# Starting the input projection in two halves of the channels, on six open sums

## The reference, cut to what matters

```python
mod = (jax.nn.silu(c) @ w_ada[l] + b_ada[l])[:, None, :]
sh_m, sc_m, g_m, sh_f, sc_f, g_f = jnp.split(mod, 6, axis=-1)
h = rmsnorm(x, norm_mix_w[l]) * (1.0 + sc_m) + sh_m
z, xbc, dt, q, k, v = jnp.split(h @ w_in, SPLITS, axis=-1)
```

## Time and profile before

| | us |
|---|---|
| median of three runs | 1695.97 |
| the profiled execution | 1696.15 |
| its span in the trace | 1694.4 |
| TensorE busy in the span | 1593.2 |
| the first matmul of the projection starts at | 62.93 |
| the first matmul of unit 2 starts at | 95.56 |

### The profile page before, as it was taken

One profiled execution on the slowest core, in us unless ns is written; L12 is line 12 of the kernel. 1 busy time (PEld: TensorE's weight loads), 2 busy tenths in 40 slices (PEclk: granted clock), 3 DMA queues, 4 the chain that ended last, 5 costly groups with the idle time before them and its releaser, 6 DMA issues.

```text
span 1694.4 us, 23175 instructions
## 1 busy us (share of the span) xinstructions
PE 1593.2 (94%) x9153; PEld 1412.9 (83%) x9153; DVE 994.3 (59%) x1603; ACT 651.8 (38%) x1143; POOL 453.6 (27%) x274
## 2 busy tenths in 40 slices
PE   4899998899998888789999999999999999999996
PEld 3689897689996666668899999999889989989875
DVE  3765416732115777654776666666466687667834
ACT  4531223321114666644332232224444454445532
POOL 0121124332201000365743333333621121112232
PEclk8899999899999999999999999999999999999998
DMA  9545110231214222327522222222364435544442
GB/s 326 198 163 199 38 28 1 57 89 38 67 53 155 101 101 77 124 87 205 203 68 67 66 62 63 63 78 73 99 188 124 133 103 167 160 135 122 149 164 70
DMA packets 163858, 189.09 MB, mean 112 GB/s; under 512 B 7851, under 2 KB 126868, under 8 KB 163731
## 3 DMA queue, kind: packets, MB, share of 16 engines
q1 hardware_dynamic: 148074, 148.89, 28.1%
q10 hardware_dynamic: 10300, 21.01, 4.1%
q0 software_dynamic: 5376, 17.71, 3.0%
HBM read 170.48 MB, written 17.11 MB: 111 GB/s over the span
## 4 chain that ended last, share of the span: by engine, by line
PE 81%; DVE 10%; ACT 3%; issue 3%; DMA 2%; POOL 1%; ACTq 0%; DVEq 0%; SPq 0%; POOLq 0%
PE PS L727 17%; PE PS L728 16%; PE PS L729 16%; PE PS L1188 4%; PE PS L1190 4%; PE PS L1189 4%; PE PS L650 4%; PE PS L1117 2%; PE PS L1118 2%; PE PS L1119 2%; PE PS L1046 2%; PE PS L985 2%; DVE y_new L1666 1%; PE PS L740 1%; DMA weights_raw<-in_w_up_dram 1%
## 5 line engine op out<-in xcount | busy, mean ns | idle before, releaser
L2347 POOL TENSOR_TENSOR weights_lo<-weights_raw,weights_hi 128x1024 fp32r<-128x1024 f32 x103 | 267.6, 2601 | 696.4 <-ACT weights_hi L1876 532.3
L727 PE MATMUL PS<-h_hi,weights_hi 128*128 128x384 f32 x1280 | 433.9, 339 | 3.3 <-DVE h_lo L1279 2.9
L728 PE MATMUL PS<-h_lo,weights_hi 128*128 128x384 f32 x1280 | 431.4, 337 | 0.0
L729 PE MATMUL PS<-h_hi,weights_lo 128*128 128x384 f32 x1280 | 431.3, 337 | 0.0
L1876 ACT ACTIVATE weights_hi<-weights_raw 128x1024 fp32r<-128x1024 f32 x202 | 213.2, 1058 | 159.1 <-PE PS L1190 97.5
L727 PEld LDWEIGHTS PS<-h_hi,weights_hi 128*128 128x128 f32 x1280 | 241.7, 189 | 11.9 <-issue 11.7
L728 PEld LDWEIGHTS PS<-h_lo,weights_hi 128*128 128x128 f32 x1280 | 241.7, 189 | 0.1
L729 PEld LDWEIGHTS PS<-h_hi,weights_lo 128*128 128x128 f32 x1280 | 241.6, 189 | 0.0
L1188 PE MATMUL PS<-weights_hi,g_hi 128*128 128x512 f32 x396 | 159.3, 402 | 8.9 <-POOL g_lo L2485 5.5
L1190 PE MATMUL PS<-weights_hi,g_lo 128*128 128x512 f32 x396 | 157.4, 397 | 0.0
L1189 PE MATMUL PS<-weights_lo,g_hi 128*128 128x512 f32 x396 | 156.6, 396 | 0.0
(11 more groups left out here) (389 smaller groups left out, 2465.3 us busy)
## 6 DMA issues: line engine op xcount, KB each, us to landing
weights_raw<-in_w_up_dram SPq DMA_DIRECT2D x88, 512.0 KB, 3.9
weights_raw<-in_w_down_dram SPq DMA_DIRECT2D x66, 512.0 KB, 4.4
w_ada_unit<-in_w_ada_dram SPq DMA_DIRECT2D x32, 512.0 KB, 5.4
weights_raw<-in_w_in_dram SPq DMA_DIRECT2D x24, 512.0 KB, 5.4
weights_raw<-in_w_out_dram SPq DMA_DIRECT2D x24, 512.0 KB, 4.0
w_ada<-in_w_ada_dram SPq DMA_DIRECT2D x4, 2048.0 KB, 16.7
k_cache<-in_cache_k_dram SPq DMA_DIRECT2D x8, 1024.0 KB, 7.7
v_cache<-in_cache_v_dram SPq DMA_DIRECT2D x8, 1024.0 KB, 5.5
```

The lines of the kernel that those rows point to most:

```text
L727: pe.matmul(out, wh, xh, start=(i == 0), stop=False)
L728: pe.matmul(out, wh, xl, start=False, stop=False)
L729: mm = pe.matmul(out, wl, xh, start=False, stop=(i == n - 1))
L2347: mark(gp.tensor_tensor(WL[n % 3][:, :], WR[:, n % 3, :], WH[n % 3][:, :].bitcast(F32), ALU.subtract), "w_lo")
```

## The change

- Units 0 and 1 are computed by a new `first_units(g, half)`: for each block k of half the channels the three matmuls of unit 0 and the three of unit 1, waiting for each h_lo block by its own count (`MOD_NO`). So six sums are open at once, in six banks (`FIRST_BANKS`), and are completed in a second pass over channels 512 to 1023.
- The products and sums of quarters 2 and 3 (`ada_products(2)`, `(3)`, `ada_sum(2)`, `(3)`) stand between the three groups of the first half and no longer before all of the projection. `late_pair(0)` to `(3)` stand in the second half.
- The products of quarters 0 and 1 stand among the last turns of x: after the seventh and after the ninth tile.
- VectorE copies the first tile out before it scales tiles 3 to 5, and three tiles (1 to 3), no longer two, before it scales the last three.
- Modulation goes half by half over all groups on both engines, the sample tile too in two halves of the channels. `w_hi(2)` stands between the halves.

```diff
+            for j in range(6):
+                x_turn(j)
+            pe.wait_ge(*once("cond_T"))
+            setup_turns()
+            x_turn(6)
             ada_products(0)
+            x_turn(7)
+            x_turn(8)
             ada_products(1)
-            pe.wait_ge(sem("xT_dve"), NT)
-            pe.wait_ge(sem("xT_act"), NT)
             ada_sum(0)
             ada_sum(1)
-            ada_products(2)
-            ada_products(3)
-            ada_sum(2)
-            ada_sum(3)
...
+            def first_units(g, half):
...
+                for k in HALVES[half]:
+                    if g < 2:
+                        pe.wait_ge(sem("mod_lo"), MOD_NO[g, k])
+                    elif k == 4 * half:
+                        pe.wait_ge(sem("mod_lo"), MOD_NO["sample", half])
+                    for n in range(2):
...
+                        pe.matmul(bank, WH[n][:, ws], HH[:, k, cols], start=(k == 0), stop=False)
+                        pe.matmul(bank, WH[n][:, ws], HL[:, k, cols], start=False, stop=False)
+                        mm = pe.matmul(bank, WL[n][:, ws], HH[:, k, cols], start=False, stop=(k == KT - 1))
...
+            first_units(0, 0)
+            ada_products(2)
+            first_units(1, 0)
+            ada_sum(2)
+            ada_products(3)
+            first_units(2, 0)
+            ada_sum(3)
+            first_units(0, 1)
             late_pair(0)
             late_pair(1)
-            for g in range(NG):
-                in_group(0, g)
-                in_group(1, g)
-                if g < 2:
-                    late_pair(2 + g)
+            first_units(1, 1)
+            late_pair(2)
+            first_units(2, 1)
+            late_pair(3)
...
             x_norm(0)
+            x_out(0)
             x_norm(1)
-            for j in range(3):
+            for j in range(1, 4):
                 x_out(j)
             x_norm(2)
...
-            x_turned_out(0)
+            for j in range(3):
+                x_turned_out(j)
             x_stats(2)
-            x_turned_out(1)
-            x_turned_out(2)
+            for j in range(3, 8):
+                x_turned_out(j)
             w_hi(0)
+            x_turned_out(8)
             w_hi(1)
```

More of the change, by code:

```diff
@@ L461, in build, with proj_bank @@
         HALVES = [range(4), range(4, KT)]
-        MOD_ACT = [[(g, k) for g in range(NG) for k in HALVES[0]],
-                   [(g, k) for g in range(2) for k in HALVES[1]], [(2, k) for k in HALVES[1]]]
-        MOD_DVE = [[(0, k) for k in HALVES[0]], [(1, k) for k in range(2)], [(0, k) for k in HALVES[1]],
-                   [(1, k) for k in range(2, KT)], [(2, k) for k in range(KT)]]
-        MOD_HI = {gk: i + 1 for i, gk in enumerate(sum(MOD_ACT, []))}
-        MOD_LO = [[i for i, (g, _) in enumerate(sum(MOD_DVE, [])) if g == group][-1] + 1 for group in range(NG)]
-        MOD_LO[2] += 1
+        MOD_BLOCKS = [(g, k) for half in range(2) for g in list(range(NG)) + ["sample"]
+                      for k in (HALVES[half] if g != "sample" else [half])]
+        MOD_NO = {gk: i + 1 for i, gk in enumerate(MOD_BLOCKS)}
+        FIRST_BANKS = [0, 1, 2, 7, 5, 6]
+        ADA_BANKS = [4, 5, 4, 3]
+        def proj_bank(q):
+            return FIRST_BANKS[q] if q < 6 else q % 3
         SUMMED = [MIXED.index(("d", 0, FT - 1)), MIXED.index(("d", 0, 2 * FT - 1))]
@@ L734, in late_pair @@
                 pe.wait_ge(sem(f"pair_in{i % 2}"), 32 * (i // 2 + 1))
-                if i % 4 == 0 and i:
-                    pe.wait_ge(sem("ada_row"), 4 + i // 4)
+                if i % 4 == 0:
+                    pe.wait_ge(*((sem("ada_row"), 4 + i // 4) if i else (sem("ada_sum_out"), 4)))
                 for t in range(2):
@@ L1265, in scale_cols, with modulate @@
                                             op0=ALU.add, op1=ALU.mult), name)
-            def modulate(blocks):
-                for g, k in blocks:
+            def modulate(g, ks):
+                for k in ks:
                     n = 3 if g < 2 else 2
@@ L1279, in modulate, with modulate_sample, sample_lo @@
                     mark(ve.tensor_scalar(lo, x, SCOL[:, 0, k, 0:1], None, ALU.add), "mod_lo")
+            def modulate_sample(half):
+                ks = slice(4 * half, 4 * half + 4)
+                x4 = XIN[:, NPT, ks, :].rearrange("p k (b t) -> p k b t", b=NB)
+                ch(ve.tensor_tensor(x4, x4, AM[:, ks, 1:NCOND].unsqueeze(3).to_broadcast([P, 4, NB, TS]), ALU.mult))
+                out(ve.tensor_tensor(x4, x4, SCOL[:, 0, ks, 1:NCOND].unsqueeze(3).to_broadcast([P, 4, NB, TS]), ALU.add),
+                    "mod_sample")
+            def sample_lo(half):
+                ks = slice(4 * half, 4 * half + 4)
+                ve.wait_ge(sem("mod_hi"), MOD_NO["sample", half])
+                mark(ve.tensor_tensor(HL[:, ks, SEQ:T], XIN[:, NPT, ks, :], HH[:, ks, SEQ:T].bitcast(F32), ALU.subtract),
+                     "mod_lo")
             x_norm(0)
+            x_out(0)
             x_norm(1)
-            for j in range(3):
+            for j in range(1, 4):
                 x_out(j)
             x_norm(2)
-            for j in range(3, 6):
-                x_out(j)
+            x_out(4)
+            x_out(5)
             setup_cols()
-            for j in range(6, NT):
-                x_out(j)
+            x_out(6)
             ada_row(0)
+            x_out(7)
+            x_out(8)
             ada_row(1)
@@ L1916, in h2_split, with modulated_hi @@
                 mark(ac.activation(FH[0][:, :, jj * P:(jj + 1) * P], N2R[0][jj][:, :, :], ACT.Copy), "h_hi")
-            def modulated_hi(blocks):
-                for g, k in blocks:
+            def modulated_hi(half):
+                for g, k in [(g, k) for g in range(NG) for k in HALVES[half]]:
                     n = 3 if g < 2 else 2
```

91 lines of the change are left out of this document (50 added, 41 removed).

## The result

The changed kernel took 1693.97 us (median of 13 runs, 1689.55 to 1699.11), the kernel before 1696.99 beside it (13 runs, 1694.97 to 1698.92). The ratio is 0.9976, with an interval of 0.9967 to 0.9985: 2.5 to 5.6 us faster, 4.1 in the middle (the two medians alone lie 3.0 apart). The forecast was 1690.8 and a gain of 5.2. The sign and the size held. The gain measured is 1.1 and 1.8 us under the forecast, but both intervals take in 5.2, so the times alone do not show that anything is missing. The landmarks of the traces do, and they say where. Of the 3.2 us between 1690.8 and 1693.97 another 1.0 is the kernel before itself, which took 1696.99 here and 1695.97 where the forecast started.

A forecast was written before the change was run, and what follows sets the result against it. TensorE, busy for 94% of the span, was taken as the bound: unit 2 starting at 90.4 instead of 95.56 takes 5.2 us off 1696.15, giving 1690.95, or 1690.8 for the median; range 1687.3 to 1694.6.

The forecast's parts named there:

- The turns of x: Setup up to the second product: sixth tile's turn ends 5.45 us earlier, at 27.6; second product ends at 38.4, not 43.85.
- Rival (1): Clock stays at 1.2 GHz up to the second product, which ends at 43.4, not 38.4: 5.0 us lost, 1695.8; chance 0.12.
- First modulation: From the second product's end to the first h_lo block: 4.9 us as before, so the projection starts at 43.3 to 43.4.
- weighed rule: GpSimd forming weights_lo slows a VectorE modulation piece beside it by 1.5 us; no overlap taken at 42, else 1692.3.
- First half: Projection over the first half of the channels: slow first 13 matmuls (3.9 us), group 0 to 49.2, sum 3 ends at 63.3.
- Rival (4): TensorE kept at 1.2 GHz through the projection's first half, costing 13 us: 1704; chance 0.06.
- Second half: Behind sum 3: added TensorE wait of 2.9 us to 66.2, then a slow start, group 0 taking 5.8 us to 72.0.
- rival (3): Clock still 2.4 GHz when the second half begins, saving 1.6 us (1689.2); fast from the seventh tile, another 1.6 (1687.6); chance 0.10.
- Group 0's end to pair 3: Second half's remaining groups and late pairs 0 to 3: from 72.0 to pair 3's end at 84.6.
- The tail: Pair 5 loads only after pair 3's use, landing 4.9 us later at 89.5; unit 2 starts at 90.4, against 95.56.
- rival (2): Pair 5 lands late behind queued loads, some 3 us, or GpSimd slows VectorE at 42 by 1.5: 1693 to 1693.8; chance 0.12.

The follow-up runs named there:

- again: The changed kernel unaltered, run and traced a second time: 1691.74 us, ratio 0.9980 to the kernel before.
- pairs_early: Changed kernel with late pairs 0 and 1 ahead of group 0's second half, pairs 2 and 3 a group forward: 1688.58 us, 0.9953 of the kernel before.
- warm_gap: Changed kernel with 13 unread matmuls in TensorE's wait before the second half: 1692.79 us, ratio 0.9967 to the kernel before.
- pairs01_only: Changed kernel with only late pairs 0 and 1 moved ahead of group 0's second half: 1692.97 us, ratio 0.9974 to the kernel before.
- both_early: Changed kernel with the edits of sum3_early and pairs_early joined: 1687.86 us, ratio 0.9939 to the kernel before.
- turns_only: Kernel before with only the new order of turns, products and copies, without the two halves: 1694.17 us, ratio 0.9985 to the kernel before.
- warm_first: Changed kernel with 5 unread matmuls on constants in TensorE's first wait, behind sums 0 and 1: 1692.75 us, ratio 0.9969 to the kernel before.
- sum3_early: Changed kernel with sum 3 between the second and third block of group 2's first half: 1690.34 us, ratio 0.9956 to the kernel before.
- both lo runs: Changed kernel with weights_lo of units 0 and 1 on VectorE: alone (lo_on_vector, 1692.94 us) and joined with sum3_early and pairs_early (1684.20 us).
- lo_on_vector: Changed kernel with weights_lo of units 0 and 1 formed by VectorE, not GpSimd: 1692.94 us, ratio 0.9971 to the kernel before.

## Why the prediction was right, and where it was off

The argument was that TensorE has no idle time between unit 2 and the end that this change touches, so that what unit 2 starts earlier comes off the time. That holds: in all twelve rows of the table the gain by the ratio is within 2.5 us of what unit 2 starts earlier in the one execution that was traced, and the two grow together. What was off is the instant of unit 2: 90.4 predicted, 93.48 and 92.08 found. By the prediction's steps (instants of the changed kernel's trace, of again's in brackets):

- *The turns of x.* Third statistics 26.1 predicted, 25.82 found; the sixth turn 27.6, found 27.0 (26.2); second product's end 38.4, found 38.54 (37.65). The instant came out, but the trade behind it did not: that is luck. I had taken the same 8.0 us for the seventh tile to the second product, one slow product paid by two fast turns. It took 9.35 (29.19 to 38.54): the slow product cost 1.8 more, and the three turns, 1.97 + 2.03, saved only 0.5 of their 4.48. The stretch began 1.2 us before the 30.4 predicted, as the sixth turn and the setup's transposes were both shorter, and the two errors cancel. Rival (1) fell.
- *First modulation.* 43.4 predicted, 44.47 (43.57) found, that is 5.9 us behind the product, not 4.9. This term was mis-sized. In the weighed rule I had looked for GpSimd's work (37.5 to 42.1) against VectorE's first piece, found it just past, and forgot the scale instruction ahead of it, which is on the same path. The 4.9, read from the earlier trace rows, held 0.56 for it; it took 1.44, 0.9 more. Most of the rest is that I ended the 4.9 at VectorE's next instruction (44.23 here), 0.24 before TensorE's first matmul. The price of the weighed rule was wrong as well. 1.5 us was one case: the instruction is held until GpSimd's ends, so the price is what is left of that one, 0.36 us for this instruction in the kernel before, 1.24 here and 1.75 in pairs_early. The Trainium skill (GPSIMD Engine Reference, 1. Specifications) names which instructions collide, those of two SBUF inputs among them. The trace agrees for this pair: L1288, with one input in PSUM, kept its 0.20 at 40.53 while L1295 behind it took 1.44.
- *First half.* From the first projection matmul to sum 3's end 19.9 predicted (43.4 to 63.3), 20.3 found (44.47 to 63.78 + 0.95). The slow start was as priced: 6.17 for group 0, 5.8 predicted. Rival (4) fell: the clock rose at 48.4 and stayed through the products and sums.
- *Second half.* The wait of 2.9 us was 2.70, and the clock did fall, but in another place than I had it. The condition of rival (3) was met, since at 67.44 TensorE started at the full clock; its 1.6 us did not come. It ran six matmuls, the last five 0.17 apart, and then fell to 1.2 GHz from 69 to 72 (0.98 in the stretch 68 to 69). The price was the same, 6.06 us for group 0 against 5.8; warm_gap and pairs_early put it at 1.3.
- *Group 0's end to pair 3.* 72.0 to 84.6 predicted, 73.50 to 87.05 found, 0.95 more. Two waits for pairs 2 and 3 (0.20 and 0.56) had no place in the sum: I counted pair 5's load and not that the queue as a whole starts again only at 74.62. Pair 2, a unit of weights and pair 3 are then issued one behind the other up to 77.1, and pair 3's second part landed at 85.9, 9.4 us behind its issue.
- *The tail.* 5.8 us from pair 3 to unit 2 predicted, 6.43 (6.26) found. The mechanism was right, and pairs01_only and pairs_early separate it: pair 5 waits for pair 3's use. It landed 5.4 us after that and not 4.9. The 4.3 of the earlier trace rows is the middle of a pair's two parts; in the kernel before they took 3.9 and 4.75, and the second one sets the time, here 5.0 behind its own issue at 87.47. The late row's 0.81 lies inside that time.

Together 1.07 + 0.4 + 0.1 + 0.95 + 0.6 = 3.1 us, the whole of 93.48 - 90.4. It is rival (2) in part: pair 5 came late by 0.6 us, and GpSimd held VectorE, though another instruction than the one named there. In the changed kernel's profiled execution a further part was given back later: unit 2 came 2.1 us earlier, but the time fell by 0.8 only (1696.15 to 1695.37). Up to the scores the lead had grown to 3.2 us (516.02 against 519.27). The attention phase (from the first matmul of the scores to the first of the output projection) then took 184.8 us against 182.8 before and 181.8 in again. The stretches 650 to 660, of the changed kernel and of again:

```profile
650.00:660.00 10.00, 8.40 (x88) 6.62 (x91) 6.83 (x15) 4.38 (x13) 0.00 (x0) 0.83 0.04 7
```

```profile
650.00:660.00 10.00, 8.07 (x98) 5.86 (x99) 7.17 (x18) 6.44 (x19) 0.00 (x0) 1.00 0.28 97
```

The same code, give or take 4 us, had a clock of 0.83 in one execution and 1.00 in the other. In the thirteen traces that phase took 181.8 to 183.0 us in ten, and 184.8, 185.0 and 186.1 in those of the changed kernel, warm_gap and both_early, whose edits do not touch it. The stretch from unit 2 to the scores differs as much (422.0 to 425.5). Such differences may be part of why the 13 runs of the changed kernel spread over 9.6 us; they put gains of 2 us at unit 2 at the edge of what the times show. What decides on it stays open.

Also open: why the clock in the stretch 28 to 34 was 0.50 to 0.54 in the traces of the changed kernel, again, turns_only, pairs01_only and warm_first, 0.72 in pairs_early, and 1.00 in those of warm_gap, sum3_early, both_early and both lo runs, all with the same instructions up to there. Just ahead TensorE waits for ScalarE's copy, before the sixth tile's second half. That wait was 0.92 to 1.37 us in the five traces with 1.00 and 1.46 to 2.21 us in the six others. It is an order without an exception in eleven traces, but no run changed that wait on purpose, so it isn't shown to be the cause. Where the clock was 1.00, the second product waited for quarter 1 (0.80 us in warm_gap) and ended at 35.5 to 36.2. This is the second part of rival (3), fast from the seventh tile on, and the product comes 2.4 to 3.0 us earlier by it, not 1.6. But in the three of these five runs that leave weights_lo on GpSimd, VectorE's first piece was held by GpSimd as well (1.82 us in warm_gap), and of 2.7 us won there at the product 1.9 reached the first projection matmul (42.58).

## What to carry to other kernels

Where work is split in two so that the first part can start early, ask what stands behind the second part's release: here the added wait cost 2.7 us of idle time, 1.3 us of clock and, since the buffers' users had moved behind it, 16 us without a load. Fill such a wait with work that is ready and whose use frees buffers (pairs_early: 3.9 us by the two ratios, for moving four calls). Go through every instruction on the released path, small ones too, when another engine's work may fall beside it: one of 36 columns took seven times its 0.20 us. And before a gain at a landmark is put down to an edit, look at the landmark just ahead of the edit: 2.05 of sum3_early's 6.0 us were there already, and 2.06 of lo_on_vector's 2.7 came without its edit in sum3_early.
